# Sparse attention over a learned top-k: the mask enters in PSUM on TensorE, one VectorE operation adds the bias and takes the extreme value

## The reference, cut to what matters

```python
score = jnp.where(causal, einsum(relu(q_idx @ k_idx.T / 8), w_idx), -inf)
_, sel = lax.top_k(score, 128)                      # per query
logits = einsum('bthc,btjc->bthj', q, kv_sel) * (KV_LATENT ** -0.5)
logits = logits + rel_bias[t5_bucket(t - sel)]
logits = jnp.where(sel <= t, logits, -inf)
p = softmax(logits); o = einsum('bthj,btjc->bthc', p, kv_sel)
```

## Time and profile before

| | |
|---|---|
| median of 3 runs | 3176.9 us (3175.44 to 3177.62) |
| the profiled execution: its own time, its span | 3174.9 us, 3173.1 us |
| granted TensorE clock, mean over the span | 0.958 |
| TensorE busy | 2792.5 us (88%) |
| VectorE busy | 1108.2 us (35%) |
| ScalarE busy | 719.0 us (23%) |
| the attention loop | 2252 to 2401.5 us of the span |

### The profile page before, as it was taken

How to read it: one execution, slowest core, us unless ns; L and a number is a source line. 1 busy time by engine, 2 the same in 40 slices (tenths; PEclk the granted TensorE clock), 3 DMA queues, 4 the chain that set the end, 5 groups by cost and what they waited for, 6 DMA issues and landing times.

```text
span 3173.1 us, 51516 instructions
## 1 busy us (share of the span) xinstructions
PE 2792.5 (88%) x21144; PEld 2126.5 (67%) x21144; DVE 1108.2 (35%) x2198; ACT 719.0 (23%) x1256; POOL 109.1 (3%) x175
## 2 busy tenths in 40 slices
PE   6999999999899999996878778989878868787787
PEld 6888874755788887875666666754446746666666
DVE  4555633222522354334211111336475341111113
ACT  3212430242322243122100000220464310000003
POOL 0000001000000000000000000000000000000000
PEclk8999999999899999997999999989899889999998
DMA  6655333111232232220699999442100109999980
GB/s 227 195 186 172 133 112 119 58 67 40 80 106 84 95 100 91 81 93 1 278 422 422 422 422 422 150 160 66 40 1 27 80 25 377 422 422 422 422 371 27
DMA packets 205505, 590.08 MB, mean 186 GB/s; under 512 B 9265, under 2 KB 133361, under 8 KB 156001
## 3 DMA queue, kind: packets, MB, share of 16 engines
q1 hardware_dynamic: 202832, 575.47, 47.3%
q0 software_dynamic: 2288, 12.39, 1.2%
q10 hardware_dynamic: 288, 0.89, 0.1%
HBM read 586.58 MB, written 7.38 MB: 187 GB/s over the span
## 4 chain that ended last, share of the span: by engine, by line
PE 69%; DMA 21%; DVE 6%; ACT 2%; issue 2%; SPq 1%; DVEq 0%; ACTq 0%
PE bank L1627 32%; DMA ring<-in_exp_w 20%; PE bank L1934 8%; PE bank L2009 4%; PE bank L1780 4%; PE bank L1749 3%; PE bank L1908 2%; PE bank L1994 2%; PE bank L1586 2%; PE bank L1738 1%; PE bank L1828 1%; PE bank L1567 1%; PE bank L1601 1%; SPq L450 1%; DMA ring<-in_w_ada 1%
## 5 line engine op out<-in xcount | busy, mean ns | idle before, releaser
L1627 PE MATMUL bank<-parts 128*128 128x512 f32 x3008 | 939.5, 394 | 29.4 <-DVE parts L993 17.3
L1627 PEld LDWEIGHTS bank<-parts 128*128 128x128 f32 x3008 | 568.2, 190 | 149.5 <-issue 28.7
L1934 PE MATMUL bank<-ring,arena 128*64 128x256 f32 x4096 | 497.6, 393 | 177.8 <-DMA ring<-in_exp_w 177.1
L1627 PE MATMUL bank<-parts,ring_low 128*128 128x512 f32 x1504 | 589.7, 392 | 0.0
L1934 PEld LDWEIGHTS bank<-ring,arena 128*64 128x64 f32 x4096 | 330.2, 136 | 308.6 <-issue 202.9
L1627 PEld LDWEIGHTS bank<-parts,ring_low 128*128 128x128 f32 x1504 | 285.4, 190 | 60.0
L987 DVE TENSOR_TENSOR ring_low<-ring,parts 128x2048 fp32r<-128x2048 f32 x96 | 215.2, 2245 | 195.5 <-ACT parts L642 195.3
L1952 PEld LDWEIGHTS bank<-arena,ring 128*64 128x64 f32 x8192 | 266.2, 138 | 16.4 <-ACT arena L620 1.1
L1402 DVE SCALAR_TENSOR_TENSOR arena<-arena,bank 128x128 f32<-128x128 f32 x128 | 44.3, 346 | 656.2 <-ACT arena L762 656.2
L1952 PE MATMUL bank<-arena,ring 128*64 128x64 f32 x8192 | 263.3, 222 | 0.7 <-ACT arena L620 0.7
L620 ACT ACTIVATE arena<-bank 128x128 f32<-128x128 f32 (+2 forms) x228 | 92.1, 407 | 688.3 <-PE bank L1941 247.3
(11 more groups left out here) (286 smaller groups left out, 2471.4 us busy)
## 6 DMA issues: line engine op xcount, KB each, us to landing
ring<-in_exp_w SPq DMA_DIRECT2D x384, 1024.0 KB, 10.3
ring<-in_w_ffn_in SPq DMA_DIRECT2D x44, 1024.0 KB, 5.5
ring<-in_w_ada SPq DMA_DIRECT2D x36, 1024.0 KB, 5.3
ring<-in_w_ffn_out SPq DMA_DIRECT2D x20, 1024.0 KB, 5.0
ring<-in_w_in SPq DMA_DIRECT2D x18, 1024.0 KB, 5.1
ring<-in_conv_w_in SPq DMA_DIRECT2D x12, 1024.0 KB, 5.1
ring<-in_attn_w_in SPq DMA_DIRECT2D x10, 1024.0 KB, 9.4
ring<-in_attn_w_out SPq DMA_DIRECT2D x8, 1024.0 KB, 5.0
```

Of the source, the lines that this page charges most:

```text
L1627: i = mm(o, a[:, cols[0], cols[1]], b, start=first_ and n == 0, stop=last_ and n == 2)
L1934: x = mm(bank[s][64 * f:64 * f + 64, 0:2 * P].rearrange("p (w n) -> p w n", w=2), XW[:, s, k], ring[:, 3 * s:3 * s + 2, c0:c0 + 2 * P - 1: ...
```

## The change

Five things change.

1. The query tiles `Q2` are written with the factor `-LATENT ** -0.5`, by the same ScalarE instruction.
2. The bias rows `VB` are written negated, by a `tensor_scalar` in place of a copy.
3. The masks become fp32r tiles of 0 or +1e30 (`MASK`, `CAUSAL`), with an fp32r identity (`IDENT`). They lie where `QI` was. That is five VectorE operations in place of three, on a new semaphore `mask`.
4. TensorE adds the mask: behind the fp32 product of a unit comes a product of `IDENT` with the mask tile into the same bank, `n` columns wide.
5. VectorE's three operations of a unit become one `tensor_tensor_reduce` that adds the negated bias and takes the minimum, which is the negated row maximum. ScalarE's exponential gets `scale=-1.0`. The next logits into a bank wait for `att_max` in place of `att_s`.

```diff
+        MASK = rounded(18944, 3, SEQ)
+        CAUSAL = rounded(20480, 1, P)
+        IDENT = rounded(20608, 1, P)
...
-                evac(Q2[:, h], bank[4 + h % 4][:], "q2")
+                A_(Q2[:, h], bank[4 + h % 4][:], ACT.Copy, scale=-LATENT ** -0.5).then_inc(sem("q2"), 1)
...
-                    A_(S2[:, i % 3, 0:n], S2[:, i % 3, 0:n], ACT.Exp, bias=DS[:, i:i + 1],
+                    A_(S2[:, i % 3, 0:n], S2[:, i % 3, 0:n], ACT.Exp, scale=-1.0, bias=DS[:, i:i + 1],
...
-            nc.vector.tensor_copy(VB[0:HEADS2, 0:512], bank[6][0:HEADS2, :]).then_inc(sem("vb"), 1)
-            nc.vector.tensor_copy(VB[0:HEADS2, 512:640], bank[7][0:HEADS2, 0:P]).then_inc(sem("vb"), 1)
+            TSc(VB[0:HEADS2, 0:512], bank[6][0:HEADS2, :], -1.0, None, ALU.mult).then_inc(sem("vb"), 1)
+            TSc(VB[0:HEADS2, 512:640], bank[7][0:HEADS2, 0:P], -1.0, None, ALU.mult).then_inc(sem("vb"), 1)
...
+            TSc(CAUSAL[:, 0], causal, -1.0, None, ALU.mult).then_inc(sem("mask"), 1)
+            nc.vector.tensor_copy(IDENT[:, 0], ident).then_inc(sem("mask"), 1)
             for qb in range(1, TT):
-                acc = SM[:, qb - 1, 0:(qb + 1) * P]
-                st.did(TSc(acc, acc, TAKEN / 2, NEG, ALU.is_gt, ALU.mult))
-            st.wait()
+                n = (qb + 1) * P
+                TSc(MASK[:, qb - 1, 0:n], SM[:, qb - 1, 0:n], TAKEN / 2, -NEG, ALU.is_gt, ALU.mult)\
+                    .then_inc(sem("mask"), 1)
...
-                    STT(out=S, in0=bank[i % 2][:, 0:n], scalar=LATENT ** -0.5, in1=TOE[:, h, SEQ - n:SEQ],
-                        op0=ALU.mult, op1=ALU.add).then_inc(sem("att_s"), 1)
-                    dve.wait_ge(sem("att_s"), ATT["s"] + i + 1)
-                    seq(TTn(S, S, causal if qb == 0 else SM[:, qb - 1, 0:n], ALU.add))
-                    nc.vector.tensor_reduce(DS[:, i:i + 1], S, AXX, ALU.max, negate=True).then_inc(sem("att_max"), 1)
+                    nc.vector.tensor_tensor_reduce(S, bank[i % 2][:, 0:n], TOE[:, h, SEQ - n:SEQ], 1.0, 3.0e38,
+                                                   ALU.add, ALU.min, DS[:, i:i + 1]).then_inc(sem("att_max"), 1)
...
-                    pe.wait_ge(sem("att_s"), ATT["s"] + u - 1)
-                mm(bank[u % 2][:, 0:n], Q2[:, h, qb * P:qb * P + P], CKVT[:, 0:n], start=True, stop=True)\
+                    pe.wait_ge(sem("att_max"), ATT["max"] + u - 1)
+                mm(bank[u % 2][:, 0:n], Q2[:, h, qb * P:qb * P + P], CKVT[:, 0:n], start=True, stop=False)
+                mm(bank[u % 2][:, 0:n], IDENT[:, 0], MASK[:, qb - 1, 0:n] if qb else CAUSAL[:, 0], start=False, stop=True)\
                     .then_inc(sem("att_mm"), 1)
...
+            pe.wait_ge(sem("mask"), 5)
```

## The result

| | before | after |
|---|---|---|
| median | 3176.5 us (3175.4 to 3177.6) | 3145.2 us (3141.8 to 3147.0, 4 runs) |
| ratio to before | | 0.990, 95% interval 0.9883 to 0.9917 |
| profiled execution: its own time, its span | 3174.9, 3173.1 us | 3145.9, 3144.1 us |
| first VectorE operation of the attention | 2252.6 | 2255.0 |
| from it to the last output copy | 148.9 us | 117.4 us |

The kernel is 31.3 us faster, 1% of its time; 24.6 were forecast. All of it was won in the attention: 31.4 us there (148.86 less 117.43), nothing behind.

A forecast was written before the change was run, and what follows sets the result against it. Attention was taken as held by a two-unit loop through three engines; savings 7.1 + 8.2 + 6.2 + 3.5 + 1.2 - 0.2 - 1.4 = 24.6 us took the profiled 3174.9 to 3150.3, median 3152.3, range 3145 to 3162.

The forecast's parts named there:

- The loops worked out for full clock: Attention blocks 1 to 3: two units would take 3.09, 4.02 and 4.98 us, from 3.87, 5.03 and 6.19.
- the change of precision: TensorE, mask product: switching to fp32r inside a bank's fp32 group costs nothing that shows.
- The half-rate rival: VectorE's fused operation runs at half rate, 0.53 us more at 512 columns: 3161 us; chance 0.1.
- the exposed product: Mask product exposed or below fp32r speed, 0.35 us more per unit on TensorE: 3168 us; chance 0.07.
- The masks in front of the loop: Building masks and identity, less than 3 us, costs nothing: VectorE had been idle 55.66 us there.
- if it ends at the same moment: Lower clock ends when it did before, so more of block 1 runs at 1.2 GHz: a loss of 1.4 us.
- block 0's loop of 2.79 at 1.2 GHz: Block 0: two units fall from 3.23 to 2.79 us, 1.40 a unit, saving 3.5 us.
- a sign of being wrong: A lower clock ending much before or behind 2279 us would make the forecast wrong.
- the first rival: TensorE's clock rises sooner in block 0: 3146 us for all of it, 3149 for half; chance 0.2.
- the 0.20 us for a mask product of 128 columns at the lower clock: Block 0: the mask product adds 0.2 us to the loop, because the weight load shows.
- I take 2.62: Block 3: TensorE's own unit with the mask, 2.61 to 2.66 us, exceeds the loop's 2.49; saves 7.1 us.
- last unit, start: Attention's ends: the last unit alone gives about 1.2 us; the mask delays the first unit by 0.2.

The follow-up runs named there:

- the filler run: Kernel before, plus one fp32 product of 128 columns into an unused bank in turns 2 to 15 of TensorE's loop: 3175.2 us.
- the kernel before with the logits ahead: Kernel before, with the logits issued one unit earlier in TensorE's queue: 3162.0 us, ratio 0.9956.
- the zero product: Kernel before, plus the identity product over a tile of zeros, the three VectorE operations kept: 3180.0 us.
- the kernel with the logits ahead: Changed kernel, with the logits issued one unit earlier in TensorE's queue: 3136.0 us, ratio to before 0.9876.
- two reorderings: Changed kernel with logits one unit earlier in TensorE's queue, 3136.0 us; then also VectorE's output copy one turn later, 3130.8 us.

## Why the prediction was right and wrong

**Right: the loop.** The loops worked out for full clock were 3.09, 4.02 and 4.98 us for two units in blocks 1 to 3; measured 3.09, 4.03 and 4.99. The steps that carry them held one by one: 0.725 us for each VectorE operation removed (4.75 without a mask product to 5.48 with the mask on VectorE), 0.12, 0.17 and 0.23 for the mask product (none, one and two), nothing for the change of precision, 692 ns for the fused operation. The half-rate rival and the exposed product are out. The masks in front of the loop cost no time, and nothing behind it took any back.

**Wrong: the clock.** The step that failed is "if it ends at the same moment", which took 1.4 us off, and with it block 0's loop of 2.79 at 1.2 GHz. The clock was back after 3.4 us, at 2260.9 and not near 2279, which the prediction itself had named as a sign of being wrong. Block 0 gave 7.4 us, not 3.5, and block 1 6.2, not 4.8. That was the first rival, to which I gave 0.2 and 3146 for all of it. That the kernel came at 3145.2 is in part luck: of the 6.4 us that the rival adds, the clock gave 5.3 (3.9 in block 0, 1.4 in block 1), and block 3, for the other reason below, gave another 1.3. The rows for and against it stood in the text, but I weighed the 23.4 us of block 0 before as evidence against it, although the very thing that the change alters is how dense the work in that block is. Nor was the 88% that TensorE's records covered there any evidence: in the filler run the clock came back from a stretch with 94%, and in the kernel before with the logits ahead it stayed low for 20 us at 94%. The filler run shows that work added to the old block 0 can bring the clock back; the zero product shows that not any added work does. What exactly the clock answers to was not found out and stays open.

In the same step, the 0.20 us for a mask product of 128 columns at the lower clock was too much: the zero product, with the clock low through block 0, added 0.10 to the loop there (3.33 against 3.23).

**Wrong: TensorE's own unit.** The step "I take 2.62" for block 3. It came from 2.43 between transposes in the earlier trace rows plus 0.23. TensorE's whole unit with the mask is 2.42 to 2.43 (the timeline with two mask products less one; the one with the logits ahead), so the unit before was 2.2, and more than 0.2 of the 2.43 was not work of its own. I had allowed 0.05 for a wait, from 0.454 us for an fp32 pass of 512 columns; two passes take 0.86, not 0.91. In the earlier trace rows the logits, the transposes and the value product take 0.96, 0.49 and 0.98; with TensorE never waiting, in the kernel with the logits ahead, their shares are 0.87, 0.44 and 0.89 (its 2.43 less 0.23 for the mask). The first difference is the wait for ScalarE; why the other two go with it is not shown. The loop, 2.49, stayed the bound, and block 3 gave 8.4 us, not 7.1.

| | forecast | measured |
|---|---|---|
| block 0 | 3.5 | 7.4 |
| block 1, with the clock's part | 6.2 - 1.4 | 6.2 |
| block 2 | 8.2 | 7.9 |
| block 3 | 7.1 | 8.4 |
| last unit, start | 1.2 - 0.2 | 1.4 |
| sum | 24.6 | 31.4 |

The measured column begins at the first VectorE operation, so the 0.2 of the start is not in it; the rounded parts add up to 31.3.

## What to carry to other kernels

When engines work in turns on different units, find the loop first: one period of the timeline, from an operation back to itself, and how many units it spans. What an edit is worth is what it takes off that loop divided by the units, and the queue order of an engine can be the longest part of it: here two reorderings gave another 14 us. Where a stage runs at the lower clock of TensorE, price both clocks for the stage after the change, because a shorter loop packs its work more densely; a change that has this effect wins twice, as block 0 did here (7.4 us for 3.5).

## What the runs showed of the hardware that was not expected

Adding one useless fp32 product of 128 columns to 14 of the 16 turns of a stage made the stage 3.2 us faster (21.6 against 24.8), with TensorE's clock back after 3.4 us in place of 23.4; an fp32r product of the same width, over zeros, did not bring it back (24 us at the lower clock). The two differ in kind, in place and in data, and no run here separates these. An fp32r product into a PSUM group that an fp32 product opened costs 0.23 us at 512 columns, like any other. VectorE's fused operation, add then minimum with one source in PSUM, runs at the speed of a plain addition, 692 ns for 512 columns; its accumulator read of 83 ns does not show in the loop.
